# The first attention of a 14-stage network: head-group queries first, in two half-row slabs of 512 columns, and new load and work orders around them

## The reference

```python
hn = rms_norm(h, norm_mix_g[0])
proj = hn @ ab_w_in                      # 1024 x 2304
qa, ka, va, qb, kb, vb = split(proj)     # 512, 128, 128, 512, 512, 512 columns
qa = apply_rope(rms_norm(qa per head of 64), cos, sin)   # 8 heads
ka = apply_rope(rms_norm(ka per head of 64), cos, sin)   # 2 heads
o_a = softmax(qa ka^T / 8) va            # 4 query heads per key head
o_b = dilated attention of qb, kb, vb with a relative bias, 8 heads
h = h + concat(o_a, o_b) @ ab_w_out
```

## Time and profile before

| | us |
|---|---|
| median of 3 runs | 1609.76 (1609.74 to 1609.76) |
| the profiled execution, its own time | 1610.46 |
| its span, first to last instruction | 1608.4 |
| PE busy | 1601.1 |
| DVE busy | 1050.6 |
| ACT busy | 852.7 |
| POOL busy | 45.7 |

### The profile page before, as it was taken

The page is one execution under the profiler, slowest core; times in us unless marked ns, Lnnn a source line. Parts: engine busy times, 40 slices in busy tenths (PEclk is TensorE's granted clock), DMA queues, the critical chain, the costliest instruction groups (busy, mean ns, idle before and its releaser), DMA issues.

```text
span 1608.4 us, 22435 instructions
## 1 busy us (share of the span) xinstructions
PE 1601.1 (100%) x8645; PEld 1353.1 (84%) x8645; DVE 1050.6 (65%) x1215; ACT 852.7 (53%) x1069; POOL 45.7 (3%) x50
## 2 busy tenths in 40 slices
PE   9999999999999999999999999999999999999999
PEld 7878888978888888888888888888888888888887
DVE  6866656877656776667777666766667554566665
ACT  6654444785444554446776444554445554554453
POOL 2100000000000030000100000000000000000000
PEclk9999999999999999999999999999999999999999
DMA  9635455524555465445345555455455444445540
GB/s 354 229 119 216 178 207 185 167 104 168 200 207 186 154 222 202 189 181 186 132 169 197 209 183 186 167 209 203 189 180 199 164 176 174 166 156 192 202 183 26
DMA packets 42854, 294.26 MB, mean 183 GB/s; under 512 B 4784, under 2 KB 5344, under 8 KB 8736
## 3 DMA queue, kind: packets, MB, share of 16 engines
q1 hardware_dynamic: 39312, 281.04, 47.5%
q0 software_dynamic: 3184, 12.02, 2.3%
q10 hardware_dynamic: 288, 0.20, 0.0%
HBM read 289.18 MB, written 3.15 MB: 182 GB/s over the span
## 4 chain that ended last, share of the span: by engine, by line
PE 98%; DMA 1%; DVE 1%; ACT 0%; issue 0%; SPq 0%; DVEq 0%
PE ups L293 26%; PE accs L260 15%; PE accs L261 15%; PE accs L262 15%; PE ups L296 13%; PE accs L293 2%; PE ups L498 1%; PE accs L296 1%; PE ups L1448 1%; PE accs L449 1%; PE accs L446 1%; PE accs L451 1%; DMA raw<-weights 1%; PE ups L2501 1%; PE ups L1069 1%; PE ups L1058 1%
## 5 line engine op out<-in xcount | busy, mean ns | idle before, releaser
L245 DVE TENSOR_TENSOR wlo<-raw,whi 128x2048 fp32r<-128x2048 f32 x263 | 603.9, 2299 | 214.9 <-ACT whi L241 214.7
L293 PE MATMUL ups<-xhl,whi 128*128 128x512 f32 x1824 | 572.8, 395 | 0.0
L241 ACT CAST whi<-raw 128x2048 fp32r<-128x2048 f32 x265 | 505.5, 1910 | 106.1 <-PE accs L262 105.1
L296 PEld LDWEIGHTS ups<-xhl,wlo 128*128 128x128 f32 x1824 | 342.6, 188 | 80.3
L296 PE MATMUL ups<-xhl,wlo 128*128 128x256 f32 x1824 | 358.3, 278 | 0.0
L293 PEld LDWEIGHTS ups<-xhl,whi 128*128 128x128 f32 x1824 | 282.4, 189 | 5.0
L260 PE MATMUL accs<-whi,hidh 128*128 128x512 f32 x692 | 272.2, 393 | 0.0
L261 PE MATMUL accs<-wlo,hidh 128*128 128x512 f32 x692 | 269.7, 390 | 0.0
L262 PE MATMUL accs<-whi,hidl 128*128 128x512 f32 x692 | 269.4, 389 | 0.0
L262 PEld LDWEIGHTS accs<-whi,hidl 128*128 128x128 f32 x692 | 129.9, 188 | 27.7
L260 PEld LDWEIGHTS accs<-whi,hidh 128*128 128x128 f32 x692 | 129.9, 188 | 24.3 <-issue 0.7
(11 more groups left out here) (274 smaller groups left out, 1401.9 us busy)
## 6 DMA issues: line engine op xcount, KB each, us to landing
raw<-weights SPq DMA_DIRECT2D x265, 1024.0 KB, 4.8
gain<-gains POOLq DMA_DIRECT2D x9, 512.0 KB, 4.0
rel_scratch<-sub_rstd POOLq DMA_DIRECT2D x1, 2048.0 KB, 9.9
big<-rel_scratch POOLq DMA_DIRECT2D x1, 1536.0 KB, 7.8
h<-x_in SPq DMA_DIRECT2D x2, 512.0 KB, 5.2
raw<-weights SPq DMA_DIRECT2D x2, 512.0 KB, 6.6
tabs<-consts POOLq DMA_DIRECT2D x1, 1024.0 KB, 6.5
big<-big POOLq DMA_DIRECT2D x2, 384.0 KB, 4.8
```

Source lines behind the costliest of these rows:

```text
L241: nc.scalar.copy(whi[:, m % SPLIT, :], raw[:, m % RAW, :]).then_inc(hi_ready, 1)
L245: nc.vector.tensor_tensor(wlo[:, m % SPLIT, :], raw[:, m % RAW, :], whi[:, m % SPLIT, :].bitcast(F32), ALU.subtract).then_inc(lo_ready, 1)
L293: mm = nc.tensor.matmul(bank, W(whi, n, k, j * P, (j + 1) * P), xhl[:, k, :, :].rearrange("p a n -> p (a n)"), start=k == 0, stop=False)
L296: mm = nc.tensor.matmul(bank[:, 0:T], W(wlo, n, k, j * P, (j + 1) * P), xh[:, k, :], start=False, stop=k == KC - 1)
```

## The change

1. Slabs 0 and 1 are now the two `row_slabs` of all 512 query columns (features 0 to 511, then 512 to 1023); slab 2 is k and v; slabs 3 to 8 are as before. `first_block` and `second_slab` are replaced by `first_queries`, with matmuls of 512 columns into two banks.
2. x is loaded in four quarters by halves of the features. The first goes by ACT's queue, `first_in` by SP's. Slab 1, too, comes in two halves. The rope's angles are asked for by ACT after its casts of slab 1, POOL's tables after slab 1's halves.
3. The blocks of x are transposed in the order 0, 2, 1, 3, each just before or between the products.
4. The kinds are normed in the order q0, q1, k and turned in the order q0, k, q1. q1 has buffers of its own for squares and unit vectors.
5. PE's list has half a product more before `turn(0)`, and each later half stands one place earlier; the lists of ACT and DVE follow. The loop of DVE's list shown above is not changed.

The core of the diff:

```diff
+        def first_queries(pe):
+            def part(m, t, ks, sides, last=False):
+                for k in ks:
                     act, weight = (xl if sides == "lh" else xh), (wlo if sides == "hl" else whi)
+                    mm = nc.tensor.matmul(accs[:, t, :], act[:, 4 * m + k, t * P:(t + 1) * P],
+                                          W(weight, m, k, 0, 2 * IN_W, 2 * IN_W),
+                                          start=m == 0 and k == 0 and sides == "hh", stop=last and k == 3)
                 return mm
+            turn_part(pe, 0, 0)
             pe.wait_ge(xh_ready, 1)
+            pe.wait_ge(S("half0"), 17)
+            part(0, 0, (0, 1), "hh")
             pe.wait_ge(xl_ready, 1)
+            part(0, 0, (0, 1), "lh")
+            turn_part(pe, 0, 2)
+            pe.wait_ge(S("half0"), 18)
+            part(0, 0, (0, 1), "hl")
+            pe.wait_ge(hi_ready, 1)
+            part(0, 0, (2, 3), "hh")
+            part(0, 0, (2, 3), "lh")
+            turn_part(pe, 0, 1)
+            pe.wait_ge(lo_ready, 1)
+            part(0, 0, (2, 3), "hl")
             pe.wait_ge(xh_ready, 2)
+            part(0, 1, range(4), "hh")
+            part(0, 1, range(4), "hl")
+            turn_part(pe, 0, 3)
             pe.wait_ge(xl_ready, 2)
+            part(0, 1, range(4), "lh").then_inc(slab_used, 1)
+            pe.wait_ge(xh_ready, 3)
+            pe.wait_ge(S("half1"), 17)
+            part(1, 0, (0, 1), "hh")
+            pe.wait_ge(hi_ready, 2)
+            part(1, 0, (2, 3), "hh")
...
@@ raw_scalar (ACT)
-                first_high(act, 0)
+                first_high(act, 0, 0)
+                first_high(act, 0, 1)
                 act.wait_ge(xh_ready, 1)
-                first_side(act, (1,))
-                first_high(act, 1)
-                first_side(act, (2, 3))
-                split_high(act, n + 1)
+                first_side(act, (2, 1, 3))
+                first_high(act, 1, 0)
+                first_high(act, 1, 1)
+                act.dma_start(tabs[:, 0:T], consts[:, C_TAB:C_TAB + T]).then_inc(S("rope_loaded"), 16)
...
+                square_piece(act, s, 0)
+                split_high(act, n + 2)
+                square_piece(act, s, 1)
+                square_piece(act, s, 2)
@@ norm_vector (DVE)
                 first_rest(dve, (0,))
+                first_low(dve, 0, 0)
+                first_low(dve, 0, 1)
+                first_rest(dve, (2, 1, 3))
                 dve.sem_inc(xn_ready, len(PIECES))
+                first_low(dve, 1, 0)
+                first_low(dve, 1, 1)
+                split_low(dve, n + 2)
                 raw_stats(dve, s)
@@ ab_tensor (PE)
+            first_queries(pe).then_inc(slab_used, 1)
+            pe.wait_ge(lo_ready, n_ab + 3)
+            project_tokens(n_ab + 2, ab_bank(2), blocks=(0,))
             table_tensor(pe)
...
+            project_tokens(n_ab + 2, ab_bank(2), blocks=(1,)).then_inc(slab_used, 1)
             turn_kind(0)
+            piece(3, 0)
             turn_kind(1)
+            piece(3, 1)
             scores(0)
+            piece(4, 0)
             pe.wait_ge(S("row_root"), 1)
             turn(0)
             for c in range(1, 6):
                 scores(c)
                 turn(2 * c - 1)
-                piece(3 + c, 0)
+                piece(3 + c, 1)
                 if c == 1:
                     values(0)
                     turn_kind(2)
-                piece(3 + c, 1)
-                if c == 5:
+                if c < 5:
+                    piece(4 + c, 0)
+                else:
+                    ...
+                    out_piece(0, blocks=(0,), halves=(0,))
                     scores(6)
                 if c >= 2:
                     values(c - 1)
                 turn(2 * c)
@@ ab_scalar (ACT)
             raw_root_scalar(act, 0)
             square(0)
+            square(1)
             root(0)
             high(3)
             root(1)
             high(4)
+            square(2)
+            v_copy(2, va, P)
             take(0)
+            root(2)
+            high(5)
             take(1)
@@ ab_vector (DVE)
             sums(0)
             sums(1)
+            normed(0)
             dve.wait_ge(S("rope_ready"), 4)
             roped(0)
+            normed(1)
             low(3)
             sums(2)
+            normed(2)
+            roped(1)
+            low(4)
             dve.wait_ge(S("rel_loaded"), 48)
             table_vector(dve)
             front(0)
             front(1)
-            normed(2)
             back(0)
             back(1)
-            low(4)
@@ SP
+            sp.dma_start(first_in[:, :], columns[:, G_ALL:G_ALL + KC + P]).then_inc(mats_loaded, 16)
             sp.dma_start(raw[:, 0, 0:SLAB // 2], ...)
+            sp.dma_start(h[:, 1, lower], x[0, P:T, lower]).then_inc(x_loaded[2], 16)
             sp.dma_start(raw[:, 0, SLAB // 2:SLAB], ...)
+            sp.dma_start(h[:, 0, upper], x[0, 0:P, upper]).then_inc(x_loaded[1], 16)
+            sp.dma_start(h[:, 1, upper], x[0, P:T, upper]).then_inc(x_loaded[3], 16)
+            sp.dma_start(raw[:, 1, 0:SLAB // 2], ...)
+            sp.dma_start(raw[:, 1, SLAB // 2:SLAB], ...)
@@ ACT's block, first instruction
-            act.dma_start(first_in[:, :], columns[:, G_ALL:G_ALL + KC + P]).then_inc(mats_loaded, 16)
+            act.dma_start(h[:, 0, 0:D // 2], x[0, 0:P, 0:D // 2]).then_inc(x_loaded[0], 16)
```

More of the change, by code:

```diff
@@ L185, in program @@
         slab_used = sem("slab_used")
-        x_loaded = [sem(f"x_loaded{t}") for t in range(TB)]
+        x_loaded = [sem(f"x_loaded{b}") for b in range(2 * TB)]
         gain_loaded = sem("gain_loaded")
@@ new lines, in first_queries @@
+            pe.wait_ge(xh_ready, 3)
[3 more added lines that the diff above has]
+            part(1, 0, (2, 3), "hh")
+            pe.wait_ge(xl_ready, 3)
+            part(1, 0, range(4), "lh")
+            pe.wait_ge(S("half1"), 18)
+            part(1, 0, (0, 1), "hl")
+            pe.wait_ge(lo_ready, 2)
+            part(1, 0, (2, 3), "hl", last=True)
+            pe.wait_ge(xh_ready, 4)
+            part(1, 1, range(4), "hh")
@@ L438, in first_wide @@
+            part(1, 1, range(4), "hl")
+            pe.wait_ge(xl_ready, 4)
+            return part(1, 1, range(4), "lh", last=True)
         def first_wide(pe, n, q):
@@ L1122, in ab_tensor @@
                 turn(2 * c)
-            pe.wait_ge(lo_ready, n_abo + 1)
-            pe.wait_ge(S("ab_plain"), 4)
             pe.wait_ge(S("ab_v"), 3)
-            pe.wait_ge(S("att_o_low"), 2)
-            out_piece(0, blocks=(0,), halves=(0,))
+            out_piece(0, blocks=(0,), halves=(1,))
             turn(11)
-            out_piece(0, blocks=(0,), halves=(1,))
             out_piece(0, blocks=(1,)).then_inc(slab_used, 1)
@@ L1209, in ab_scalar @@
             square(0)
-            high(2)
-            v_copy(0, va, P)
+            square(1)
             root(0)
-            square(1)
             high(3)
@@ L1216, in ab_scalar @@
             high(4)
+            square(2)
+            v_copy(2, va, P)
             take(0)
-            square(2)
+            root(2)
+            high(5)
             take(1)
-            high(5)
-            root(2)
             bring_table(ACT.Exp)
@@ L1274, in roped @@
             def roped(i):
[L1275 to L1276 removed]
+                kind = TURNS[i]
                 g = GROUPS[kind]
                 w = g * HD
[L1279 to L1280 removed]
+                unit, (cross, dst) = unit_of(kind), (by_head(tok_view(tile, kind)) for tile in (cross_tok, roped_tok))
+                dve.wait_ge(S("ab_normed"), KINDS.index(kind) + 1)
                 if i >= 1:
@@ L2955, in pack @@
     wq = w[:, 0:512].reshape(D, A_HEADS, HD)[:, a_order].reshape(D, 512)
-    part = list(in_slabs(np.concatenate([wq, w[:, 512:]], axis=1)))
-    slabs += [part[k] for k in (2, 0, 1, 3, 5, 4, 6)] + list(row_slabs(w[:, 1792:2304]))
+    part = list(in_slabs(w[:, 512:1792]))
+    slabs += [*row_slabs(wq), *(part[k] for k in (0, 1, 3, 2, 4)), *row_slabs(w[:, 1792:2304])]
     w = i["ab_w_out"][0]
```

135 lines of the change are left out of this document (56 added, 79 removed).

## The result

| | before | after |
|---|---|---|
| median, us | 1609.80 (1609.74 to 1610.49, 6 executions) | 1618.44 (1617.06 to 1619.15, 6 executions) |
| profiled execution, its own time | 1610.46 | 1617.06 |
| its span | 1608.4 | 1615.0 |

The ratio is 1.0051, with an interval of 1.0039 to 1.0063: 8.6 us slower. The forecast was +4.5, with an upper end of +7.5; sign and place were right, the size was not.

A forecast was written before the change was run, and what follows sets the result against it. PE, busy 1601.1 of 1608.4 us, was taken as the bound, so early losses carry to the end. +1.0 up to turn(0) and +3.5 at piece(5,0) gave +4.5 on the median 1609.76: 1614.3 us, range 1611.8 to 1617.3.

The forecast's parts named there:

- Part 1: Kernel start: with less of x to land, the first matmul comes at 7.15 instead of 8.18, -1.0 us.
- part 3: First two slabs: PE stands from 14.9 to 16.3 behind ACT's cast, later 0.4 more, +1.85 us; slabs end at 22.3.
- Part 2: Products of q0 and q1: 48 matmuls of 512 columns instead of 96 of 256, -0.6 us.
- Part 4: Slab 2: PE waits 0.4 us before it, the table is needed at 25.7, and the slab ends at 30.3.
- Part 5: DVE's order up to turn(0): list done at 34.0 to 34.3, turn(0) at 41.4, balance +1.0 us (bounds -0.5 and +2).
- PE waits 0.4 to 0.7 for turn_kind(1): Before k's transposes: PE stands 0.4 to 0.7 us until DVE has roped k.
- The nine terms of DVE's list: DVE's work from 22.65 on, statistics through the rope of k, given as ending at 34.0.
- Part 6: Before piece(5,0), near 48 to 52: PE waits for DVE's low(5), at least 3.35 us, 3.5 taken.
- the lower end of the forecast's two: POOL's rope of q1: 2.9 us without blocking by DVE, making the wait before piece(5,0) 3.35 us, not 3.95.
- Late in the attention: nothing: Late attention: out_piece(0) one step earlier needs low(9), made one round before, so it costs nothing.
- a difference that arises after 60 us: A listed sign that the forecast is wrong: a difference between the kernels arising later than 60 us.
- Rival 3: PE's clock rises later at the start or falls in the long wait: +1.2 to +3 us more, 1615.5 to 1617.3; 15%.
- the rest, 68%: Chance left for the forecast itself, after the rivals; its own range 1613.0 to 1615.8.

The follow-up runs named there:

- experiment 9: Kernel before with the new loads alone (x's first block in two halves, columns on SP's queue, POOL's tables later): 1610.87 us, ratio 1.0005.
- experiment 4: Changed kernel with 14 matmuls over zeros, result unread, added to PE's list in the standstill before piece(5,0): 1616.82 us, ratio 1.0044.
- experiment 2: Changed kernel with ACT's cast of slab 1's first half ahead of the last first_side, DVE's lists following: 1618.17 us, ratio 1.0050.
- experiment 3: Changed kernel with the edits of both experiment 1 and experiment 2: 1613.14 us, ratio 1.0019.
- experiment 1: Changed kernel with DVE's low(5) moved right after the second probabilities, ahead of round c = 1: 1613.39 us, ratio 1.0021.
- experiment 5: Changed kernel with PE's halves of products back in their old places, everything else of the change kept: 1613.94 us, ratio 1.0025.
- Experiment 8: experiment 5 with the cast order of experiment 2 and the rope table asked for early: 1612.92 us, ratio 1.0019.
- experiment 6: Kernel before with the new places of PE's halves alone, and low(4) as far forward as in the change: 1616.13 us, ratio 1.0039.
- experiment 7: experiment 3 plus piece(3,1) before turn_kind(1), rope table asked for after slab 0's casts, one vb copy before the cast: 1612.18 us, ratio 1.0013.
- experiment 10: experiment 9 with two more warm-up matmuls of zeros between the first four transposes and the first product: 1611.41 us, ratio 1.0011.

## Why the prediction was right or wrong

**Part 1, the start: right in place, wrong in worth.** 7.06 against 7.15. But experiment 9 shows that an early first matmul alone is worth nothing: there the next input, the second weight half, is the bound, and it was not moved. In the changed kernel it was: ACT casts it from 8.65 on (9.62 before), and PE is through with the first slab at 14.96 instead of 15.5. The gap of part 3 then takes that.

**Part 2, wider matmuls: right.** 4 of them start 0.91 apart (18.79, 19.70): 0.2275 each. For the columns-plus-2.5-ns rule of the Trainium skill, TensorE: Matmul & The Clock Gate, "Wait — 56ns, not 53.3ns?", the trace does not agree: about 14 ns over 512 columns at 2.4 GHz here, and 13 over 256. In experiment 4, though, the bf16 matmuls of zeros come every 0.216 us, which is the rule's figure, also with a weight load for each. So it is the fp32r matmuls of this kernel that cost more.

**Part 3, the gap behind ACT's cast: right.** The last matmul before it starts at 14.73 and costs 0.23, so PE stands from 14.96 to 16.44; forecast 14.9 to 16.3. PE's end of the two slabs is 22.42, forecast 22.3. (The terms named for parts 1 to 3 add up to +0.1, not +0.2.) Experiments 2 and 3 add that narrowing it is worth 0.3 us at most, because the next wait (k) takes it: a gap of the chain is not yet a gain.

**Part 4: right in place.** The table is at 25.54 (forecast 25.7). The wait of 0.4 before slab 2 is not there: PE starts it at 22.47.

**Part 5, DVE's order: a wrong sum that came out nearly right by luck, and a table that was late in the profiled execution.** The step that failed is "PE waits 0.4 to 0.7 for turn_kind(1)": it waited 1.2, and turn(0) came at 42.01 against 41.4, +1.6 against +1.0. The nine terms of DVE's list from 22.65 on add up to 33.3, not to the 34.0 of the forecast; with the 0.5 for the tables they give 33.85, and a wait of 0.25 at most. k was ready for PE at 34.6, and PE was there at 33.5. Too short in the list are above all sum, root and normed of k, 1.64 us instead of 1.25, since DVE stands 0.55 for ACT's root; and the tables came 0.2 later. The 0.7 of the wrong sum happened to cover this.

The rest is the rope table. ACT asks for it at 14.24, before the two casts that stand ahead of it in its list have begun, and not at 17.1. Its way took 10.5 us instead of 8.5, so that it landed at 24.75 where the forecast has 25: two errors that cancel. POOL made the tables of it from 24.90 to 26.61, and DVE, there at 25.66, waited (timelines of ACT and DVE, and the issue with its us to landing):

```profile
14.24 0.33 ACTq L579 DMA_DIRECT2D tabs<-consts  x1
15.24 2.01 ACT L224 CAST whi<-raw 128x1024 fp32r<-128x1024 f32 x2
tabs<-consts ACTq DMA_DIRECT2D x1, 128.0 KB, 10.5
26.64 0.69 DVE L1303 TENSOR_TENSOR big<-big 128x512 f32<-128x512 f32 x1 [0.98 <-POOL big L2735]
```

In three other traces of the same lists of ACT and DVE up to this point, those of experiments 1, 4 and 5, the table took 9.4, 8.7 and 9.1 us to land, DVE did not wait for POOL, and PE's wait for k was 0.5:

```profile
25.66 0.69 DVE L1303 TENSOR_TENSOR big<-big 128x512 f32<-128x512 f32 x1
```

(experiment 1). With PE's order unchanged, in 1 and 4, turn(0) then came at 41.25 and 41.50, +0.9 and +1.1, which is the forecast. So 0.5 to 0.8 of the changed kernel's 1.6 belongs to the one execution that was profiled. Experiment 8, with the table early, keeps 0.5 of k's wait and the 0.9 at turn(0): there DVE's list with its wait for ACT, not the table, is the bound.

**Part 6, the standstill: right.** PE's last transposes before it start at 48.48 (arrival was forecast for 48.2), the first matmul behind it at 52.16 (51.7 to 52.15): 3.4 us of idle time, 3.7 from start to start, against 3.5. The path is the one forecast: from values(0) over o_low and back(3) to low(5), 4.0 us against 3.9. Experiment 1 removes the wait, experiment 6 makes it again in the other kernel. One reading was off, without effect on the sum: the 49.24 of the earlier trace rows is not the first matmul of piece(5,0), which starts at 48.99 in the timeline, so the old slack was 0.9 us and not 1.2. The kernel after has POOL's rope of q1 so (its timeline):

```profile
42.95 1.27 POOL L2753 TENSOR_TENSOR big<-big 128x512 f32<-128x512 f32 x1 [4.31 <-DVE xn L1347]
44.18 1.43 POOL L2755 TENSOR_TENSOR big<-big 128x256 f32<-128x256 f32 x2
```

Beside no two-input subtraction the first multiply takes 1.27 us instead of 3.17; that is the lower end of the forecast's two: POOL was done at 45.6 and held nobody. With the rule of the Trainium skill, SBUF — State Buffer, "Who interferes with whom", the trace agrees: 2.7 us for the three.

**"Late in the attention: nothing" was wrong by 0.8 us.** This step failed as well, and it put a term at nothing. I had checked low(9) for the out_piece that moves, but not the operations that now come *sooner after* what they need. values(4) waits 0.5 for ACT's two copies of vb, which stand behind a cast. From the start of scores(5) to the end of those copies it is 7.3 us (82.30 to 89.57); PE has only 6.9 us of work there now, where it had 8.2 before (74.24 to 82.45). turn(14) waits 0.2 for DVE's probabilities. Experiments 5 and 6 tie both waits to PE's order. The working of the prediction had exactly this for piece(5,0), and should have done it for every consumer down the list. It had also named "a difference that arises after 60 us" as a sign of being wrong, and 1.2 us of the 6.6 arose there.

**Rival 3, the clock, is the other miss: 15% for what happened in five of six executions.** It came on top of the forecast, not in its place. The step that failed is its chance, and that "the rest, 68%" was taken as free of it. Its price was well put (+1.2 to +3): 1.0 to 1.4 at the median, 2.1 for the slowest over the profiled one, and 2.2 by the pitches of experiment 2. That the gate closes after an idle stretch, the Trainium skill (TensorE: Matmul & The Clock Gate, "Part 1: The HAM clock gate") says; experiment 2 shows it here.

**The last 0.4 to 0.5 us are open.** From 1225.5 on the difference grows once more, at DVE's addition of the residual. DVE's timeline of the kernel after:

```profile
1225.51 1.28 DVE L750 SCALAR_TENSOR_TENSOR h<-accs,scale_out,h 128x1024 f32<-128x1024 f32 x1 [0.40 <-PE accs L262]
```

Before, it followed its predecessor without a pause. PE, named as the releaser, is not the cause: its matmul L262 that ends the product starts 0.85 us before this addition (1224.66), and 0.49 us before it in the kernel before (1218.52 and 1219.01), each at the same place in PE's work. DVE alone is late, and then PE's transposes are. It is so in every trace with the new head (experiments 1 to 5, 7 and 8) and in none with the old one (6, 9, 10), so it comes with the new head and not with the order of pieces or the loads. Between 120 and 1221 us the distances are the same; nothing that was changed works there. I have no cause for it.

**The offset.** I worked against the profiled execution, which was 0.66 above its median, and added the difference to the median. That assumed that both kernels' profiled executions stand alike to their medians; one was 0.66 above and the other 1.4 below.

In sum: forecast +4.5; + 0.6 (turn(0), most of it this execution's late table), + 0.2 (the standstill and the work about it: 5.3 - 1.6 against 3.5), + 0.8 (late waits), + 0.5 (open) = +6.6 in the spans, and 2.0 by the clock and the two offsets. The two steps that failed in the mechanism are the clock, left out of the sum, and the late waits, put at nothing; the one execution without the clock's fall, 1617.06, is inside the range.

## What to carry to other kernels

When a step of one engine is pulled forward, what it feeds on must be pulled forward on the other engines as well: go through *all* consumers down the list and ask how much work is left between each and its producer, not only for the first. Where a standstill like the ones here (3.3 to 3.5 us of idle time) is forecast on a PE that otherwise hardly pauses, the clock's fall is part of the forecast, as a second price of 1 to 2 us, not a rival to it. An earlier first matmul gains nothing if the second input comes when it always came. And before a difference of half a microsecond between two single traces is given a cause, look at a third trace of the same lists: the landing of one DMA moved turn(0) by 0.5 to 0.8 us here.

## What the runs showed of the hardware

- In the one trace that caught it, PE was idle for 3.5 us and then ran for 5.3 us of uninterrupted work at the lower clock (experiment 2). DVE was busy nearly all through the idle stretch (3.5 of 3.8 us), ACT and POOL in the first part of it. The fall is not in every execution of one kernel: the changed kernel has it in five of six, by their mean clocks.
- Matmuls of zeros in the gap keep the clock up in four of five executions (experiment 4). Near the start, two more did not help (experiment 10), and there the clock can fall after PE was idle for 1.9 us (experiment 7, 7.8 to 11.2 us); after 1.8 us in experiment 3's trace it did not.
- fp32r matmuls of 512 columns come every 0.2275 us, bf16 ones of zeros every 0.216 us (experiment 4), both with a weight load for each.
- A DMA of 128 KB on ACT's queue, asked for at 14.1 to 14.6 us while SP's queue was moving megabytes, took 8.7 to 10.5 us to land in four executions with the same lists (the changed kernel, 1, 4, 5), against 8.5 when it was asked for at 4.55.
- A DMA in ACT's list was issued at 14.24 us, 1.0 us before the first of the two casts written ahead of it began (the changed kernel; 14.13 and 15.13 in experiment 1).
